# Reordering the prologue of a two-block transformer kernel on one NeuronCore

## The reference, cut to what matters

```python
cs = jax.nn.silu(c)                                   # c: (1, 1024)
for l in range(2):
    mod = (cs @ ada_w[l] + ada_b[l]).reshape(1, 3, 3, 1024)[:, :, :, None, :]
    h = _rmsnorm(x, norm_g[l, 0]) * (1.0 + mod[:, 0, 1]) + mod[:, 0, 0]
    x = x + 0.5 * mod[:, 0, 2] * _swiglu(h, ffn_w_gate[l, 0], ffn_w_up[l, 0], ffn_w_down[l, 0])
    ...                                               # a mixer with attention, a second swiglu
```

## Time and profile before

| what | value |
|---|---|
| median of 3 runs (lowest, highest) | 2979.97 us (2975.04, 2980.57) |
| profiled execution, its span | 2976.49 us, 2974.4 us |
| TensorE matmul, weight load: busy | 2817.2 us (95%), 2508.9 us (84%) |
| VectorE, ScalarE, GpSimd: busy | 1589.6 us (53%), 599.5 us (20%), 15.6 us (1%) |
| first product of the feed-forward starts at | 40.63 us |
| sizes of the early loads: x, cond, vec, ident | 1024, 512, 316, 64 KB |
| one_hot, off_mask, iota, rel_bias, b_gates | 47.9, 35.9, 4.0, 3.0, 1.0 KB |
| one ada or up chunk; the bias table | 2048 KB; 3072 KB |

### The profile page before, as it was taken

One profiled execution on the slowest core, in us unless ns is written; L12 is line 12 of the kernel. 1 busy time (PEld: TensorE's weight loads), 2 busy tenths in 40 slices (PEclk: granted clock), 3 DMA queues, 4 the chain that ended last, 5 costly groups with the idle time before them and its releaser, 6 DMA issues.

```text
span 2974.4 us, 67823 instructions
## 1 busy us (share of the span) xinstructions
PE 2817.2 (95%) x28798; PEld 2508.9 (84%) x28798; DVE 1589.6 (53%) x3030; ACT 599.5 (20%) x1431; POOL 15.6 (1%) x27
## 2 busy tenths in 40 slices
PE   5999999999999999999999989999799999989887
PEld 4999898899999998889999867998678766867664
DVE  6776673267578567515666555889842111212113
ACT  1112113121121111321111220123521110111111
POOL 0000000000000000000000000000000000000000
PEclk8999999999999999999999999999899999999999
DMA  7665664346556557534565526782248889889995
GB/s 311 252 239 220 247 232 193 130 155 238 217 196 264 207 227 275 213 114 162 196 242 198 214 86 252 298 330 100 86 186 324 336 335 382 364 314 428 428 428 247
DMA packets 55553, 733.31 MB, mean 247 GB/s; under 512 B 6609, under 2 KB 6793, under 8 KB 10805
## 3 DMA queue, kind: packets, MB, share of 16 engines
q1 hardware_dynamic: 51364, 716.68, 60.6%
q0 software_dynamic: 3984, 13.74, 1.3%
HBM read 729.31 MB, written 4.23 MB: 247 GB/s over the span
## 4 chain that ended last, share of the span: by engine, by line
PE 82%; DMA 10%; DVE 5%; issue 2%; ACT 1%; SPq 0%; DVEq 0%; ACTq 0%
PE psum L761 36%; PE psum L852 18%; PE psum L1347 11%; PE psum L1398 5%; PE psum L839 3%; DMA work<-in_down_e_dram 3%; DMA work<-in_up_e_dram 2%; DMA ring<-in_up_dram 2%; PE psum L755 2%; PE psum L1414 1%; DMA ring<-in_w_v_dram 1%; DVE ring L1909 1%; DMA ring<-in_w_ccch_dram 1%; PE psum L1373 1%; DMA ring<-in_ada_dram 1%
## 5 line engine op out<-in xcount | busy, mean ns | idle before, releaser
L761 PE MATMUL psum<-work,ring 128*128 128x128 f32 x3680 | 440.8, 275 | 2.2 <-ACT work L1491 2.2
L761 PEld LDWEIGHTS psum<-work,ring 128*128 128x128 f32 x3680 | 425.2, 192 | 3.0 <-issue 1.6
L761 PE MATMUL psum<-work 128*128 128x128 f32 x3328 | 390.6, 276 | 3.2 <-DVE work L2003 1.9
L761 PEld LDWEIGHTS psum<-work 128*128 128x128 f32 x3328 | 381.6, 193 | 3.7 <-issue 3.2
L1909 DVE SCALAR_TENSOR_TENSOR ring<-ring,cond 128x1024 f32<-128x1024 f32 x240 | 279.3, 1220 | 84.9 <-DMA ring<-in_ada_dram 84.7
L852 PE MATMUL psum<-work,ring 128*128 128x256 f32 x1344 | 296.3, 383 | 6.3 <-DMA ring<-in_m_out_dram 4.1
L852 PEld LDWEIGHTS psum<-work,ring 128*128 128x128 f32 x1344 | 257.7, 192 | 43.5 <-DMA ring<-in_m_out_dram 4.9
L852 PE MATMUL psum<-h_t,ring 128*128 128x256 f32 x1280 | 278.9, 380 | 1.0 <-ACT h_t L1612 1.0
L852 PEld LDWEIGHTS psum<-h_t,ring 128*128 128x128 f32 x1280 | 242.6, 190 | 36.0 <-issue 3.1
L761 PE MATMUL psum<-h_t,ring 128*128 128x128 f32 x2272 | 266.6, 276 | 4.3 <-DMA ring<-in_up_dram 3.3
L761 PEld LDWEIGHTS psum<-h_t,ring 128*128 128x128 f32 x2272 | 260.0, 192 | 7.1 <-DMA ring<-in_up_dram 4.4
(11 more groups left out here) (402 smaller groups left out, 2807.3 us busy)
## 6 DMA issues: line engine op xcount, KB each, us to landing
ring<-in_ada_dram SPq DMA_DIRECT2D x60, 2048.0 KB, 8.1
ring<-in_up_dram SPq DMA_DIRECT2D x55, 2048.0 KB, 8.5
ring<-in_up_e_dram SPq DMA_DIRECT2D x32, 2048.0 KB, 9.2
work<-in_up_e_dram SPq DMA_DIRECT2D x32, 2048.0 KB, 9.8
ring<-in_down_dram SPq DMA_DIRECT2D x20, 2816.0 KB, 10.6
ring<-in_down_e_dram SPq DMA_DIRECT2D x16, 2048.0 KB, 10.0
work<-in_down_e_dram SPq DMA_DIRECT2D x16, 2048.0 KB, 11.6
ring<-in_w_qk_dram SPq DMA_DIRECT2D x12, 2048.0 KB, 8.5
```

Source lines behind the costliest of these rows:

```text
L761: mm = pe.matmul(bank(bank_of)[:, pair * P:(pair + 1) * P], w, right(i), start=(first and pair == 0 and i == 0), stop=(pair == lin.pairs - ...
```

## The change

The condition is loaded first and by SyncE, on a semaphore of its own; ada0 comes next, then x and `ident` (semaphore `x_in`), ada1, ada2, and the six other small loads come behind ada3. ScalarE copies x out of PSUM. VectorE does the additions of squares between the dot products of ada1 and those of ada2, and the bias rows after the raw tiles.

```diff
-            for dst, src in ((x_tok, dram["x"]), (ident[:, :], dram["ident"]), (vec[:, :], dram["vec"]),
-                             ... (iota8[:, :], dram["iota8"])):
-                sp.dma_start(dst, src).then_inc(small_in, 16)
+            def x_loads():
+                for dst, src in ((x_tok, dram["x"]), (ident[:, :], dram["ident"])):
+                    sp.dma_start(dst, src).then_inc(x_in, 16)
+            def small_loads():
+                for dst, src in ((vec[:, :], dram["vec"]), (one_hot, dram["one_hot"]), (off_mask, dram["off_mask"]),
+                                 (table, dram["rel_bias"]), (bgate[:, :], dram["b_gates"]), (iota8[:, :], dram["iota8"])):
+                    sp.dma_start(dst, src).then_inc(small_in, 16)
+            sp.dma_start(cond[:, :], bass.AP(dram["cond"].tensor, 0, [[0, P], [1, D]])).then_inc(first_cond_in, 16)
...
                         sp.dma_start(ring[:, slot, 0:width], src).then_inc(chunk_in[slot], 16)
+                        if p.name == "ada0" and n == 0:
+                            x_loads()
+                        elif p.name == "ada0" and n == 3:
+                            small_loads()
...
-            pe.wait_ge(small_in, 128)
+            pe.wait_ge(x_in, 32)
...
             p = place("bias_rows")
+            pe.wait_ge(small_in, 96)
...
-            act.wait_ge(small_in, 128)
-            act.wait_ge(signal["cond_in"], place("ada0").of("cond_in", 0))
+            act.wait_ge(first_cond_in, 16)
             act.activation(cond[:, :], cond[:, :], ACT.Silu).then_inc(signal["cond_set"], 1)
+            p = place("load_x")
             for b in range(LIN):
-                act.wait_ge(bank_free[b], reads(place("norm0", 0), b))
+                act.wait_ge(bank_full[b], products(p, b))
+                act.activation(x[:, 2 * b:2 * b + 2, :], bank(b), ACT.Copy).then_inc(bank_free[b], 1)
+            for b in range(LIN):
+                act.wait_ge(bank_free[b], reads(p, b) + 1)
+            act.sem_inc(signal["x_tile"], DT)
             for k in range(DT - 2):
                 square(place("norm0", 0), k)
+            act.wait_ge(small_in, 96)
             for l in steps.loop("layer", DEPTH):
...
-            dve.wait_ge(small_in, 128)
-            p = place("load_x")
-            ...                                  (VectorE's four copies of x, its waits and its x_tile)
+            def first_sums(n, i, where):
+                ada_sums(place("ada0"))(n, i, where)
+                if n == 1:
+                    for f in range(1, DT - 1):
+                        squares_so_far(place("norm0", 0), f)
+            p = place("ada0")
+            dve.wait_ge(signal["cond_set"], p.of("cond_set", 0))
+            walk(p, loop(p), None, first_sums)
+            dve.wait_ge(small_in, 96)
+            ada_next(p, (new_scale, *ada_b(0, 1, 2)), (new_shift, *ada_b(0, 0, 1)))
+            prepare(vcol("norm_g", 0, DT))
+            for f in range(DT):
+                raw_tile(f)
             p = place("bias_rows")
             dve.wait_ge(bank_full[4], products(p, 4))
             dve.tensor_tensor(bias_row[:, 0:383], psum[0:NG * HG, 4 * 512:4 * 512 + 383], off_mask,
                               ALU.add).then_inc(bank_free[4], 1)
-
-            for f in range(1, DT - 1):
-                squares_so_far(place("norm0", 0), f)
-            ...                                  (the dot products, ada_next)
             dve.wait_ge(rows_out, 16)
-            prepare(vcol("norm_g", 0, DT))
-            for f in range(DT):
-                raw_tile(f)
...
-            load_cond(0)
             pool.memset(ones[:, :], 1.0).then_inc(ones_set, 1)
```

More of the change, by code:

```diff
@@ L202, in stages @@
     prologue = {
-        "load_x": with_(uses(b0=1, b1=1, b2=1, b3=1), cond_in=16, cond_set=1, x_tile=DT),
+        "load_x": with_(uses(b0=1, b1=1, b2=1, b3=1), cond_set=1, x_tile=DT),
         "bias_rows": uses(b4=1),
@@ L608, in build @@
         small_in = sem("small_in")
+        x_in = sem("x_in")
+        first_cond_in = sem("first_cond_in")
         ones_set = sem("ones_set")
```

## The result

The changed kernel takes 2985.53 us in the median of ten runs (2980.69 to 2988.9), the kernel before 2979.73 us in ten (2975.04 to 2982.73). The ratio is 1.0021, with a 95% interval from 1.0013 to 1.003: slower by 5.8 us at the median, 3.9 to 8.9 by the interval. The interval leaves out 1, so there is a difference, and it is at the bound of 0.2% which the prediction set; the forecast was 1.7 us. One execution of the repeated changed kernel took 12,798 us, against 2978.53 to 2986.85 us for the ten others, and is left out.

What follows compares the result with a forecast made beforehand. TensorE, busy 95%, bounds the kernel; time can be won only in the serial 40.6 us prologue. The store's wait adds 1.7 us at `mean_square`, replacing the 0.85 us later start: 2979.97 + 1.7 = 2981.7 us, range 2975.5 to 2986.0.

Steps and rivals of the forecast that it cites:

- the bound of 0.2%: Whole kernel: a measurement tells 0.2%, 6 us, from no change; no difference was given 0.90.
- the 1.7 us of the sum: Whole kernel: the delay at `mean_square`, +1.7 us, in place of the 0.85 us at TensorE's start, not on top.
- The two waits: Prologue, VectorE: sixth addition waits about 6 us for the seventh square; later VectorE waits for the bias rows' store.
- two terms behind the store: Between store issue and `mean_square`: 4.5 us for the store to land, then 0.3 us until VectorE goes on.
- The deciding step: VectorE, prologue: sixth addition needs the seventh square, behind `small_in` at 30.0 us; stall about 6 us, products end at 40.25.
- TensorE's start: End of prologue: TensorE starts at about 41.5 us against 40.63, +0.85 us.
- rival B: SyncE's queue: the condition loaded first is slow, all landings come 4.8 us later; +6.5 us, 2986.5 us; chance 0.07.
- a loaded and a quiet row: Bias rows' store: 5.5 us with the DMA full, 2.3 us for a GpSimd load in a quieter stretch; 4.5 taken.
- A delay of VectorE at 47 us: From `mean_square` to the token sums: room is 0.05 us, so the whole 1.7 us come out at TensorE.
- The late expansion: Table's expansion (3,072 KB) moves from 21.5 to about 48.5 us; cost nothing, readers come at 253 us.
- rival C: Up weights' loads: the expansion takes 35 us again and slows an up chunk; +3 us more, 2984.5 us; chance 0.10.
- No difference in TensorE's clock: Prologue: TensorE idles at granted clock 0.50 from 17 to 40 us; changed kernel idles too, so no difference.

## Why the prediction was right or wrong, point by point

It said no difference that can be measured, with 2981.7 us and 2975.5 to 2986.0. The measured 2985.53 lies in that range, 0.5 us from its upper end, and the measured difference of 5.8 us, is over three times the 1.7 us of the sum and just about at the bound of 0.2%; that "no difference" and the range still fit is in part luck. The two waits and their order were right; two terms behind the store were too small.

- The deciding step, the sixth addition behind the small loads, came out as worked: small loads landed at 29.9 (30.0), dot products ended at 40.2 (40.25), VectorE's stall 5.9 us (about 6). Moving that addition removed the stall, and moving the loads cut it to 0.9 us.
- TensorE's start, 41.61 (41.5). ada0 was used from 10.38 (10) and ada1 from 17.86 (17.5). For ada0 two errors cancel: it was issued at 1.35 us and not 1.9, and took 8.9 us and not 8.1. The condition landed at 5.3 us, 4.6 after its issue: rival B didn't happen.
- The store: issued at 44.06 (43.9). Its landing was taken at 4.5 us, between a loaded and a quiet row. It took 5.3, and 5.3 to 5.6 us in all nine profiled runs that issue it behind the raw tiles, much like the 5.5 of before. That term was 0.8 us short. In each of them an up chunk was on its way beside it, though in the changed kernel the DMA share was 0.03 from 48 us on while the store landed at 49.35. No run issues it with nothing beside it, so why it takes 5.3 us stays open.
- What stands between the landing and `mean_square`: taken at 0.3 us, measured 2.1 (49.35 to 51.42). Some 0.6 us (49.38 to 49.98 in the chain) go to the semaphore waits in front of the copy that VectorE steps through once the store has landed, which lay in idle time before; 1.1 us are the small copy, held by GpSimd's descriptors. With the store issued 0.2 us later than taken, 0.8 us more of landing and these 1.8 us, the forecast delay of 1.7 us at `mean_square` becomes the measured 4.4. The hold of the copy was not in the sum at all, and it is the term that failed: the prediction looked at who would wait for the store, and not at what else the store's landing sets off at the same instant.
- A delay of VectorE at 47 us reaches TensorE whole: 4.4 us at `mean_square`, 4.3 at the landmark. Right.
- The late expansion costs nothing in the DMA: it took 23.1 us (49.65 to 72.8) in place of 35.0, no product waited for an up chunk there, and rival C didn't happen. (Its price was added up wrongly: 2981.7 and 3 more are 2984.7, not 2984.5.)
- The rule of the Trainium skill that was weighed, some 2 us for such a store (DMA: Bandwidth & Descriptors, the anatomy of one DMA on the gpsimd path), would have hidden it. The measured landings (5.3 to 5.6 us) speak against it for a store that is issued while other loads are in flight.
- "No difference in TensorE's clock" was wrong in a small way: the rise came some 3.5 us after TensorE's start in the kernel before and about 6 us after it in the kernel without the store's wait, and TensorE's new stalls can be followed by a drop.

What stays open is how the 1.5 us between the landmark's shift and the median's are divided between later clock drops and the spread of the medians.

## What to carry to other kernels

Before a load is moved back in a queue, follow each wait on its semaphore through the engines that execute in order: the additions waited for small inputs that they don't read, only because a square was issued behind a common wait. An operation moved off the path takes its store and its waits along, and if the next instruction on a critical engine waits for the store, 5 us of landing stand where there were none; another buffer removed that here. When two engines are released by the same landing, look at whether they need the same thing next.

## What the runs showed of the hardware that was not expected

- GpSimd's 1.65 us of building descriptors held an fp32 copy of 128 x 24 elements on VectorE until its end (1.29 to 1.31 in place of 0.18 us, in five traces), and left a reciprocal beside it at 1.75 us (two traces).
- A store of 36 KB to DRAM from GpSimd took 5.3 to 5.6 us to land in each of ten traces, always with a 2,048 KB load on its way when it was issued.
- Nine calls of a product whose result nobody reads, 4.2 us on an idle TensorE, saved 2.5 us of the 16 products behind them, by the clock.
- After stalls of TensorE of 1.36 and 1.84 us, and of 1.00 and 1.83 us, with 2 us of products between them, the next 32 products took 5.46 us in place of 3.83, at a granted clock of 0.50 in part; after 0.55 and 1.84 us they did not. One such drop costs 1.6 us, over a quarter of the 5.8 us that the whole change was measured at.
